# Extra gather moved in among two experts' products, a reordered end of the output stage, and latent products between two condition halves

## The chip, the core and the metric

The kernel runs on one core of one Trainium2 chip. The time is device microseconds (us) of one execution on that core, smaller is better. Before the change the median of three runs is 1278.52 us, from 1276.56 to 1280.14.

## The reference, cut to what matters

Two layers of a transformer-like block work on 256 latent tokens and 256 context tokens of width 1024. In each layer, modulation values come from a condition vector, tokens are normalised and mixed (attention and Fourier branches), and then go through a mixture of experts in which a router picks one of four groups for each token and two of its four experts:

```python
mod = silu_c @ w_ada[l] + b_ada[l]
h_lat = rmsnorm(x_lat, norm1_g[l]) * (1.0 + sc1) + sh1
...
m = g_a * (o_a @ w_br_mla) + g_b * (o_b @ w_br_na) + g_c * (o_c @ w_br_ft)
return m @ w_out
...
x_lat = x_lat + g1 * y_lat
h_lat = rmsnorm(x_lat, norm2_g[l]) * (1.0 + sc2) + sh2
x_lat = x_lat + g2 * grouped_moe(h_lat, router_w, router_bias, w_e_gate[l], w_e_up[l], w_e_down[l])
```

The second layer needs the context only as keys and values, so its output stage and its experts work on the 256 latent tokens alone.

## The kernel before

Everything is float32, and the large products are made of three products of float32r parts: each weight chunk (128 x 2048, 1 MB) is loaded by SyncE into one of five `raw` buffers, ScalarE writes the high part of half a chunk (`half_high`, L557) into one of four `w_hi` buffers, VectorE writes the low part (`half_low`, L937), and TensorE runs `three` (L1574 to L1576) on them. A high part waits until TensorE has used the half four places earlier. There is no scheduler: every engine's order is written out by hand in its own block, and engines wait for each other by semaphores. A result in PSUM lives in one of eight banks; the plan at the top gives each result its bank, and TensorE waits (`claim`) until the bank's last reader has finished.

The change touches three places of this order.

**Opening.** `condition_half` (L1661) makes half of a modulation row from one chunk of `w_ada`. `turn_rows(1)` (L1676) turns the row of the two halves of pair 1 once ScalarE has copied it; VectorE makes the modulation of blocks 2 and 3 from it. `latent(kb)` is the contraction block `kb` of the first input product: 12 products of 512 columns.

**Output stage.** Four passes `j` each make two 128-wide blocks of x. For block `kb`, VectorE adds to x (L1296) and scales a copy `xc` (L1303), ScalarE squares x (L598), and `token_block(kb)` on TensorE adds the router's logits (L1935) and transposes `xc` (L1941) into `tok` banks, for ScalarE to copy. The squares of blocks 0 to 5 are added up in `rinv` by VectorE (L953); those of blocks 6 and 7 stay in `sq`. `sums_of` (L1985) sums `rinv` and both `sq` over the features. `sum_done` is raised by the last logits, and lets ScalarE make the root `rs` (L831), from which VectorE's routing chain starts. `filler` (L2004) are products whose result nobody reads.

**Experts.** Routing puts the tokens into 4 units of 128 slots, one per group, and into extra units for tokens beyond those (3 in the first layer, 1 in the second). `n_it` is the number of experts run: 28, then 20. For expert `i`, `up(i, a)` for `a` = 0 to 3 uses half-chunk `a` (6 products of 512 columns each); then `silu` (ScalarE), `hidden` (VectorE, which scales with the token's gate `gsl`), `turn(i)` (TensorE transposes the hidden values), and `down(i)` (12 products). TensorE issues `up(i, 0)`, `turn(i - 1)`, `up(i, 1..3)`, `down(i - 1)`. The tokens of the first four units are gathered before expert 0, into `h_hi` and `h_lo`. Those of the extra units (`hx_hi`, `hx_lo`) are first read by expert 16. They are gathered in one block between experts 0 and 1:

```python
                for i in range(n_it + 1):
                    if i == 1:
                        b, was = L["row"][0]
                        claim((b, was))
                        pe.wait_ge(diag_done, l + 1)
```

In this block stand the slot numbers (L2154; ScalarE copies them to `sbr`, L894), and for each of the eight blocks `kb` of features the gathering products (L2048, and L2062 in the first layer), with the gates of one unit (L2169) behind the first `n_unit` of them. ScalarE and VectorE make `hx_hi` (L855, L856) and `hx_lo` (L1423, L1424) of each, also all eight in a row; VectorE's `unit_gates` (L1465, L1466) and `hidden(0)` (L1480) stand among them.

## Time and profile before

| | us |
|---|---|
| median of three runs | 1278.52 |
| the profiled execution, its own time | 1281.17 |
| its span, first to last instruction | 1279.5 |
| TensorE busy | 1230.6 (96%) |
| VectorE busy | 858.1 (67%) |
| ScalarE busy | 693.1 (54%) |
| mean granted TensorE clock | 0.983 |

The profiled execution took 1.67 us more than its span. Busy time of TensorE includes products at half the clock. In a timeline row the first number is the start, the second the time to the end of the last instruction, and the brackets hold the idle time of the engine ahead of it with what ended it; consecutive equal instructions are merged ("x4"). A float32 product shows as two instructions, so x8 can stand for four products of the program. PE is TensorE, PEld its weight loads, DVE VectorE, ACT ScalarE.

### The profile page before, as it was taken

The numbers are of one execution on the slowest core, as the hardware profiler recorded it, in microseconds if no ns is written. First come the engines' busy times: TensorE is split into PE (matmuls) and PEld (weight loads), VectorE is DVE, ScalarE is ACT, GpSimd is POOL, SyncE is SP. The second block draws the span as 40 slices with busy tenths as digits, with TensorE's granted clock in tenths as the row PEclk, the third lists the DMA queues.
The fourth block names the chain that finished last, engine by engine and source line by source line (L and its number), as shares of the span: only waits on it lengthen the run. The fifth ranks groups of instructions, "written<-read, shape, count | busy, mean of one in ns | idle before, by whom it ended". The sixth has DMA issues, their size and how long they took to land.

```text
span 1279.5 us, 17771 instructions
## 1 busy us (share of the span) xinstructions
PE 1230.6 (96%) x6762; PEld 978.5 (76%) x6762; DVE 858.1 (67%) x1338; ACT 693.1 (54%) x1043; POOL 15.0 (1%) x28
## 2 busy tenths in 40 slices
PE   6999999999999999999999999999899998999997
PEld 4777555688888886888888887786599986888875
DVE  4653556442444547599998996847665667899986
ACT  4432545533223344488886783536554455788863
POOL 0100000000000000000000000000000000000000
PEclk8999999999999989999999999999999998999998
DMA  9622699422222111399998993321645541899981
GB/s 364 270 88 78 234 390 338 158 99 99 99 99 99 67 66 54 122 373 371 366 364 304 349 365 127 137 99 66 264 140 190 185 145 66 323 369 369 369 305 39
DMA packets 38564, 268.98 MB, mean 210 GB/s; under 512 B 4241, under 2 KB 5393, under 8 KB 6481
## 3 DMA queue, kind: packets, MB, share of 16 engines
q1 hardware_dynamic: 37520, 263.39, 55.8%
q0 software_dynamic: 960, 4.46, 0.9%
q8 instruction: 56, 0.92, 0.3%
q14 instruction: 28, 0.22, 0.1%
HBM read 266.78 MB, written 1.05 MB: 209 GB/s over the span
## 4 chain that ended last, share of the span: by engine, by line
PE 87%; DVE 7%; ACT 2%; issue 1%; DMA 1%; SPq 0%; DVEq 0%; ACTq 0%; PEldq 0%
PE bank L1574 22%; PE bank L1576 22%; PE bank L1575 22%; PE bank L2048 3%; PE bank L1661 3%; PE bank L1841 3%; PE bank L1884 2%; PE bank L1866 2%; DVE lo L937 2%; DMA raw<-weights 1%; PE bank L1935 1%; PE bank L2143 1%; PE bank L2144 1%; PE bank L2113 1%; PE bank L1776 1%
## 5 line engine op out<-in xcount | busy, mean ns | idle before, releaser
L937 DVE TENSOR_TENSOR lo<-raw,w_hi 128x1024 fp32r<-128x1024 f32 x400 | 486.4, 1231 | 211.2 <-ACT w_hi L557 206.8
L557 ACT CAST w_hi<-raw 128x1024 fp32r<-128x1024 f32 x400 | 418.2, 1051 | 264.9 <-PE bank L1576 258.5
L1574 PE MATMUL bank<-h_hi,w_hi 128*128 128x512 f32 (+1 forms) x512 | 177.7, 347 | 4.2 <-DVE h_lo L997 2.1
L1575 PE MATMUL bank<-h_lo,w_hi 128*128 128x512 f32 (+1 forms) x512 | 176.1, 344 | 0.0
L1576 PE MATMUL bank<-h_hi,lo 128*128 128x512 f32 (+1 forms) x512 | 175.8, 343 | 0.0
L1574 PE MATMUL bank<-w_hi,h_hi 128*128 128x512 f32 (+1 forms) x320 | 126.9, 396 | 0.3 <-DVE h_lo L1424 0.2
L1576 PE MATMUL bank<-w_hi,h_lo 128*128 128x512 f32 (+1 forms) x320 | 124.4, 389 | 0.0
L1575 PE MATMUL bank<-lo,h_hi 128*128 128x512 f32 (+1 forms) x320 | 124.3, 389 | 0.0
L1574 PEld LDWEIGHTS bank<-h_hi,w_hi 128*128 128x128 f32 x512 | 97.4, 190 | 21.7 <-issue 5.9
L1576 PEld LDWEIGHTS bank<-h_hi,lo 128*128 128x128 f32 x512 | 97.4, 190 | 11.6
L1575 PEld LDWEIGHTS bank<-h_lo,w_hi 128*128 128x128 f32 x512 | 97.5, 190 | 11.0
L1574 PE MATMUL bank<-w_hi,hdT_hi 128*128 128x512 f32 x192 | 76.0, 396 | 0.0
L1575 PE MATMUL bank<-lo,hdT_hi 128*128 128x512 f32 x192 | 75.9, 395 | 0.0
L1576 PE MATMUL bank<-w_hi,hdT_lo 128*128 128x512 f32 x192 | 75.9, 395 | 0.0
L1574 PEld LDWEIGHTS bank<-w_hi,h_hi 128*128 128x128 f32 x320 | 60.7, 190 | 13.1 <-issue 1.1
L1576 PEld LDWEIGHTS bank<-w_hi,h_lo 128*128 128x128 f32 x320 | 60.6, 189 | 12.5
L1575 PEld LDWEIGHTS bank<-lo,h_hi 128*128 128x128 f32 x320 | 60.6, 190 | 11.6
L1178 DVE TENSOR_REDUCE smx<-bank 128x1 f32<-128x512 f32 (+1 forms) x72 | 42.0, 600 | 26.3 <-PE bank L1841 25.1
L755 ACT ACTIVATE prob<-bank,smx 128x512 f32<-128x512 f32 (+1 forms) x72 | 44.3, 619 | 26.3 <-DVE smx L1178 25.3
L762 ACT COPY probT<-bank 128x512 f32<-128x512 f32 x60 | 32.8, 591 | 39.0 <-PE bank L1866 39.0
L1574 PE MATMUL bank<-w_hi,hx_hi 128*128 128x512 f32 x128 | 51.9, 406 | 0.0
L1661 PE MATMUL bank<-raw,cs 128*32 128x256 f32 x768 | 48.7, 393 | 2.7 <-DMA raw<-weights 2.6
(262 smaller groups left out, 1991.9 us busy)
## 6 DMA issues: line engine op xcount, KB each, us to landing
raw<-weights SPq DMA_DIRECT2D x248, 1024.0 KB, 5.0
x<-tokens SPq DMA_DIRECT2D x4, 512.0 KB, 7.2
nab<-na_bias POOLq DMA_DIRECT2D x2, 1024.0 KB, 8.8
rp<-rope POOLq DMA_DIRECT2D x2, 512.0 KB, 4.3
ft<-dft POOLq DMA_DIRECT2D x2, 512.0 KB, 4.7
out<-x SPq DMA_DIRECT2D x4, 256.0 KB, 2.2
fd<-dft POOLq DMA_DIRECT2D x2, 128.0 KB, 5.5
vec<-vectors SPq DMA_DIRECT2D x1, 176.0 KB, 2.4
```

The lines of the kernel that those rows point to most:

```text
L557: nc.scalar.copy(w_hi[:, g % N_HI, :], raw[:, ring_slot[c], o:o + HALF]).then_inc(hi_done, 1)
L755: nc.scalar.activation(prob[:, i % 2, qb, 0:nk * P], bank[b][:, 0:nk * P], ACT.Exp, bias=smx[:, i % 2, 2 + qb:3 + qb], scale=1.0, accum_ou ...
L762: nc.scalar.copy(probT[:, i % 2, 2 * half:2 * half + 2, :], bank[b][:].rearrange("p (k q) -> p k q", k=2))\
L937: nc.vector.tensor_tensor(lo[:, ring_slot[c], o:o + HALF], raw[:, ring_slot[c], o:o + HALF], w_hi[:, g % N_HI, :].bitcast(F32), ALU.subtra ...
L1178: nc.vector.tensor_reduce(smx[:, i % 2, 2 + qb:3 + qb], bank[b][:, 0:nk * P], AX, ALU.max, negate=True)\
L1574: nc.tensor.matmul(o, l_hi, r_hi, start=start, stop=False)
L1575: nc.tensor.matmul(o, l_hi, r_lo, start=False, stop=False)
L1576: return nc.tensor.matmul(o, l_lo, r_hi, start=False, stop=stop)
L1661: ins = nc.tensor.matmul(o[32 * j:32 * j + 32, :], cs[:, w:w + N_COND], raw[:, ring_slot[p], kb * CW:(kb + 1) * CW], start=(r == 0 and hal ...
L1841: ins = nc.tensor.matmul(bank[b][:, 0:nk * P], q[:, h, t], k[:, h, k0:k0 + nk * P], start=True, stop=True)
L1866: ins = nc.tensor.transpose(bank[b][:, o:o + P], prob[:, i % 2, qb, kb * P:(kb + 1) * P], ident[:])
L2048: ins = nc.tensor.matmul(bank[b][:, 0:c1 - c0], h[:, t, kb * P:(kb + 1) * P], perm[:, t, c0:c1], start=(start and t == 0), stop=last)
```

## The change

1. Opening: `latent(0)` now stands between the two halves of condition pair 1.
2. Output stage: the sum over `rinv` moves ahead, into the last pass, between the first and the second half of its product. At the end of the stage the logits of blocks 6 and 7 and the two remaining sums come first, and the transposes of blocks 6 and 7 last.
3. Experts: the slot numbers and all gates are made during expert 0 (`beside`), and each block of the extra gather stands behind one `up(i, a)` of the experts 1 and 2. ScalarE and VectorE take their parts in the same order. The gates' bank is 5 in place of 3.

The lines of the changed kernel stand 7 to 23 lines further down, so L1935 of before is L1945 there, L1985 is L1966, L2048 is L2071. The diff, cut:

```diff
-            s["gsl"], s["row"] = results(1, [3]), results(1, [6])
+            s["gsl"], s["row"] = results(1, [5]), results(1, [6])
...
+                def extra_high(kb):
+                    b, was = L["gx"][kb]
+                    act.wait_ge(full[b], nth(b, was))
+                    shifted(hx_hi, kb, b, n_ext * P).then_inc(gxhi_done, 1)
...
+                    if i in (1, 2):
+                        extra_high(4 * (i - 1))
...
-                    more(hs[1])
-                    more(hs[2])
+                    for a in (1, 2):
+                        more(hs[a])
+                        if i in (1, 2):
+                            extra_high(4 * (i - 1) + a)
                     silu(i)
+                    if i == 0:
+                        b, was = L["row"][0]
+                        act.wait_ge(full[b], nth(b, was))
+                        nc.scalar.copy(sbr[:, 0:nq], bank[b][:, 0:nq]).then_inc(free[b], 1)
+                    if i in (1, 2):
+                        extra_high(4 * (i - 1) + 3)
                     for g in hs[3:]:
                         more(g)
...
+                def extra_low(kb):
+                    b, was = L["gx"][kb]
+                    dve.wait_ge(gxhi_done, KB * l + kb + 1)
+                    unshifted(hx_lo, hx_hi, kb, b, n_ext * P).then_inc(free[b], 1)
...
-                    if i == 1:
-                        for kb in range(KB):
-                            if kb == n_unit:
-                                unit_gates()
-                                hidden(0)
-                            b, was = L["gx"][kb]
-                            dve.wait_ge(gxhi_done, KB * l + kb + 1)
-                            unshifted(hx_lo, hx_hi, kb, b, n_ext * P).then_inc(free[b], 1)
...
-                    more(hs[1])
-                    more(hs[2])
-                    if i > 0:
-                        hidden(i)
+                    for a in (1, 2):
+                        more(hs[a])
+                        if i in (1, 2):
+                            extra_low(4 * (i - 1) + a)
+                    if i == 0:
+                        unit_gates()
+                    hidden(i)
+                    if i in (1, 2):
+                        extra_low(4 * (i - 1) + 3)
                     for g in hs[3:]:
                         more(g)
...
-                    condition(1)
+                    condition_half(1, 0)
                     latent(0)
+                    condition_half(1, 1)
                     turn_rows(1)
                     latent(1)
...
-                def token_block(kb):
-
-                    b, was = L["tok"][kb]
-                    claim((b, was))
+                def logits(kb):
+
                     if kb == 0:
                         claim((bs, wass))
                     pe.wait_ge(xc_done, KB * l + kb + 1)
...
+                def token_rows(kb):
+
+                    b, was = L["tok"][kb]
+                    claim((b, was))
                     for t in range(nt):
                         ins = nc.tensor.transpose(bank[b][:, t * P:(t + 1) * P], xc[:, kb, t * P:(t + 1) * P], ident[:])
                     ins.then_inc(full[b], 1)
+
+                def token_block(kb):
+
+                    logits(kb)
+                    token_rows(kb)
...
                         if a == 0 and j > 0:
                             token_block(2 * j - 2)
                             token_block(2 * j - 1)
+                            if j == N_OUT - 1:
+                                pe.wait_ge(acc_done, acc_from(2 * l + 2))
+                                sums_of(rinv)
                             if ns == 2 and j >= 2:
                                 shift_rows(j - 2)
                     s += 1
 
-                def sums_of(part):
-                    for t in range(nt):
-                        nc.tensor.matmul(bank[bs][:, t:t + 1], part[:, t * P:(t + 1) * P], ones[:, 0:1], start=False,
-                                         stop=False, skip_group_check=True)
-
                 n = 2 * l + 1
-                pe.wait_ge(acc_done, acc_from(n + 1))
-                sums_of(rinv)
+                logits(KB - 2)
                 pe.wait_ge(nsq_done, KB * n + KB - 1)
                 sums_of(sq[:, 0, :])
-                token_block(KB - 2)
                 pe.wait_ge(nsq_done, KB * n + KB)
                 sums_of(sq[:, 1, :])
-                token_block(KB - 1)
+                logits(KB - 1)
+                token_rows(KB - 2)
+                token_rows(KB - 1)
 
...
-                for i in range(n_it + 1):
-                    if i == 1:
-                        b, was = L["row"][0]
+                def slot_numbers():
+
+                    b, was = L["row"][0]
+                    claim((b, was))
+                    pe.wait_ge(diag_done, l + 1)
+                    for t in range(nt):
+                        ins = nc.tensor.matmul(bank[b][:, t * P:(t + 1) * P], ones[:], diag[:, t, :], start=True, stop=True)
+                    ins.then_inc(full[b], 1)
+
+                def slot_gates(units):
...
-                        claim((bg, wasg))
                         pe.wait_ge(g4_done, l + 1)
                         pe.wait_ge(permx_done, l + 1)
-                        for kb in range(KB):
-                            claim(L["gx"][kb])
-                            gather(L["gx"][kb], htok_hi, kb, 512, n_unit * P, True)
-                            gather(L["gx"][kb], htok_lo, kb, 512, n_unit * P, False)
-                            shifted(L["gx"][kb], kb, 512, n_unit * P)
-                            if kb < n_unit:
-                                for t in range(nt):
-                                    ins = nc.tensor.matmul(bank[bg][:, 8 * kb:8 * kb + 8], perm[:, t, kb * P:(kb + 1) * P],
-                                                           g48[:, t, :], start=(t == 0), stop=(t == nt - 1))
-                            if kb == n_unit - 1:
-                                ins.then_inc(full[bg], 1)
+                    for u_ in units:
+                        for t in range(nt):
+                            ins = nc.tensor.matmul(bank[b][:, 8 * u_:8 * u_ + 8], perm[:, t, u_ * P:(u_ + 1) * P],
+                                                   g48[:, t, :], start=(t == 0), stop=(t == nt - 1))
+                    if units[-1] == n_unit - 1:
+                        ins.then_inc(full[b], 1)
+
+                def gathered_extra(kb):
+
+                    claim(L["gx"][kb])
+                    gather(L["gx"][kb], htok_hi, kb, 512, n_unit * P, True)
+                    gather(L["gx"][kb], htok_lo, kb, 512, n_unit * P, False)
+                    shifted(L["gx"][kb], kb, 512, n_unit * P)
+
+                def beside(i, a):
+
+                    if i == 0 and a == 0 and ns == 2:
+                        slot_rows(1, 512, n_unit * P)
+                    if i == 0 and a == 1:
+                        slot_gates(range(n_unit - 3))
+                    if i == 0 and a == 2:
+                        slot_numbers()
+                        slot_gates(range(n_unit - 3, n_unit))
+                    if i in (1, 2):
+                        gathered_extra(4 * (i - 1) + a)
+
+                for i in range(n_it + 1):
                     for m in back_at(l, i):
                         back(m, range(4), L["back"][m])
                     if i < n_it:
                         up(i, 0)
+                        beside(i, 0)
                     if i > 0:
                         turn(i - 1)
                     if i < n_it:
-                        up(i, 1)
-                        up(i, 2)
-                        up(i, 3)
+                        for a in range(1, 4):
+                            up(i, a)
+                            beside(i, a)
                     if i == n_it:
                         for m in (4, 5):
                             back(m, range(4), L["back"][m])
```

TensorE at the end of the output stage, first layer, before: the last product of the last pass and what follows (`sq` are squares, `xc` the scaled x, `rt` routing values).

```order
L1576 MATMUL bank<-m_hi,lo 128x512
L1985 MATMUL bank<-ones,rinv 128x1 x4
L1985 MATMUL bank<-ones,sq 128x1 x4
L1935 MATMUL bank<-vec,xc 128x16 x4
L1941 MATMUL bank<-ident,xc 128x128 x4
L1985 MATMUL bank<-ones,sq 128x1 x4
L1935 MATMUL bank<-vec,xc 128x16 x4
L1941 MATMUL bank<-ident,xc 128x128 x4
L2004 MATMUL bank<-xc,ident 128x256 x5
L2015 MATMUL bank<-rt,ones 128x20
```

The changed kernel behind the last product of that pass:

```order
L1587 MATMUL bank<-m_hi,lo 128x512
L1945 MATMUL bank<-vec,xc 128x16 x4
L1966 MATMUL bank<-ones,sq 128x1 x8
L1945 MATMUL bank<-vec,xc 128x16 x4
L1956 MATMUL bank<-ident,xc 128x128 x8
L2027 MATMUL bank<-xc,ident 128x256 x5
L2038 MATMUL bank<-rt,ones 128x20
L2040 MATMUL bank<-rt,before 128x16
```

And between the two halves of its product, behind the logits of block 5 (`sh_116` are shift rows):

```order
L1945 MATMUL bank<-vec,xc 128x16 x4
L1956 MATMUL bank<-ident,xc 128x128 x4
L1966 MATMUL bank<-ones,rinv 128x1 x4
L1975 MATMUL bank<-ident,sh_116 4x128 x4
L1585 MATMUL bank<-m_hi,w_hi 128x512
```

One group of sums went ahead of the last half product, and both groups of transposes behind the last logits. TensorE from the last product of expert 0 on, second layer, before (`diag` gives the slot numbers, `g_127` the gates, `htok` the tokens):

```order
L1576 MATMUL bank<-w_hi,h_lo 128x512
L2154 MATMUL bank<-diag,ones 128x128 x2
L2048 MATMUL bank<-perm,htok_hi 128x128 x2
L2048 MATMUL bank<-perm,htok_lo 128x128 x2
L2169 MATMUL bank<-g_127,perm 128x8 x2
L2048 MATMUL bank<-perm,htok_hi 128x128 x2
L2048 MATMUL bank<-perm,htok_lo 128x128 x2
L2169 MATMUL bank<-g_127,perm 128x8 x2
```

The changed kernel, between the third and the fourth half-chunk of expert 0:

```order
L1586 MATMUL bank<-lo,h_hi 128x512
L1587 MATMUL bank<-w_hi,h_lo 128x512
L2177 MATMUL bank<-diag,ones 128x128 x2
L2189 MATMUL bank<-g_127,perm 128x8 x6
L1585 MATMUL bank<-w_hi,h_hi 128x512
```

And in expert 1, from the end of its first half-chunk on (`hid` is the hidden values of expert 0):

```order
L1586 MATMUL bank<-lo,h_hi 128x512
L1587 MATMUL bank<-w_hi,h_lo 128x512
L2071 MATMUL bank<-perm,htok_hi 128x128 x2
L2071 MATMUL bank<-perm,htok_lo 128x128 x2
L2136 MATMUL bank<-ident,hid 128x128 x2
L1585 MATMUL bank<-w_hi,h_hi 128x512
L1586 MATMUL bank<-lo,h_hi 128x512
```

The block is gone: numbers and gates stand within expert 0, and the four narrow products of a gather behind each six wide ones. VectorE at this place, second layer, before:

```order
L1424 SCALAR_TENSOR_TENSOR h_lo<-bank,mod,h_hi 128x512
L937 TENSOR_TENSOR lo<-raw,w_hi 128x1024 x4
L1424 SCALAR_TENSOR_TENSOR hx_lo<-bank,mod,hx_hi 128x128 x5
L1465 COPY gsl<-bank 128x20
L1466 TENSOR_TENSOR gsl<-gsl,bank 128x20
L1480 SCALAR_TENSOR_TENSOR hid<-bank,gsl,s_act 128x256
L1424 SCALAR_TENSOR_TENSOR hx_lo<-bank,mod,hx_hi 128x128 x3
L937 TENSOR_TENSOR lo<-raw,w_hi 128x1024
```

And in the changed kernel:

```order
L1431 SCALAR_TENSOR_TENSOR h_lo<-bank,mod,h_hi 128x512
L944 TENSOR_TENSOR lo<-raw,w_hi 128x1024 x3
L1472 COPY gsl<-bank 128x20
L1473 TENSOR_TENSOR gsl<-gsl,bank 128x20
L1492 SCALAR_TENSOR_TENSOR hid<-bank,gsl,s_act 128x256
L944 TENSOR_TENSOR lo<-raw,w_hi 128x1024 x2
L1499 TENSOR_TENSOR hdT_lo<-bank,hdT_hi 128x256
L1431 SCALAR_TENSOR_TENSOR hx_lo<-bank,mod,hx_hi 128x128
L944 TENSOR_TENSOR lo<-raw,w_hi 128x1024
L1431 SCALAR_TENSOR_TENSOR hx_lo<-bank,mod,hx_hi 128x128
```

The gates and `hid` of expert 0 moved ahead of the fourth of the low parts, and the `hx_lo` went in between later ones.

## Rows read from the trace of the kernel before

**Rows 1.** The page, part 4: the chain that ended last, by engine

```profile
PE 87%; DVE 7%; ACT 2%; issue 1%; DMA 1%; SPq 0%; DVEq 0%; ACTq 0%; PEldq 0%
```

**Rows 2.** Busy times in 50 us of experts: PE, PEld, DVE, ACT, POOL, clock, DMA

```profile
1100.00:1150.00 50.00, 50.00 (x225) 40.59 (x224) 48.24 (x54) 40.91 (x50) 0.00 (x0) 1.00 0.99 368
```

**Rows 3.** Timeline of ScalarE: silu of experts 1 and 2, second layer

```profile
1092.93 0.39 ACT L875 ACTIVATE s_act<-bank 128x256 f32<-128x256 f32 x1 [0.26 <-PE bank L1576]
1101.44 0.39 ACT L875 ACTIVATE s_act<-bank 128x256 f32<-128x256 f32 x1 [0.25 <-PE bank L1576]
```

**Rows 4.** Busy times by microsecond, end of the first layer's output stage

```profile
467.00:468.00 1.00, 1.00 (x11) 1.00 (x10) 1.00 (x2) 0.53 (x1) 0.99 (x1) 0.98 0.67 156
468.00:469.00 1.00, 1.00 (x6) 1.00 (x6) 0.18 (x1) 0.00 (x0) 0.04 (x1) 0.50 0.93 393
...
478.00:479.00 1.00, 1.00 (x7) 0.72 (x6) 0.90 (x5) 1.00 (x2) 0.00 (x0) 0.90 0.00 0
```

**Rows 5.** Timeline at the same place

```profile
465.79 0.95 PE L1985 MATMUL bank<-ones,rinv 128*128 128x1 f32 x8
...
468.79 1.09 PE L1941 MATMUL bank<-ident,xc 128*128 128x128 f32 x4
...
469.68 1.71 PE L1985 MATMUL bank<-ones,sq 128*128 128x1 f32 x8
...
473.15 0.26 ACT L831 ACTIVATE rs<-bank,eps 128x4 f32<-128x4 f32 x1 [5.62 <-PE bank L1935]
```

**Rows 6.** Timeline of the second layer's last pass and its end

```profile
1045.91 0.95 DVE L953 TENSOR_TENSOR rinv<-rinv,sq 128x256 f32<-128x256 f32 x2
...
1049.66 0.50 PE L1985 MATMUL bank<-ones,rinv 128*128 128x1 f32 x4
...
1052.17 0.26 ACT L831 ACTIVATE rs<-bank,eps 128x2 f32<-128x2 f32 x1 [1.37 <-PE bank L1935]
```

**Rows 7.** Timeline of the block between experts 0 and 1, first layer

```profile
508.46 1.06 PE L2154 MATMUL bank<-diag,ones 128*128 128x128 f32 x8
...
510.72 0.94 PE L2048 MATMUL bank<-perm,htok_hi 128*128 128x384 f32 x4 [0.50 <-ACT sbr L894]
...
515.07 0.52 PEld L2169 LDWEIGHTS bank<-g,perm 128*128 128x128 f32 x4 [0.19 <-issue]
...
515.51 0.65 PEld L2048 LDWEIGHTS bank<-perm,htok_hi 128*128 128x128 f32 x4
...
529.51 0.50 PE L1574 MATMUL bank<-w_hi,h_hi 128*128 128x512 f32 x1
```

**Rows 8.** Timeline of the block between experts 0 and 1, second layer

```profile
1073.65 4.62 DVE L937 TENSOR_TENSOR lo<-raw,w_hi 128x1024 fp32r<-128x1024 f32 x4
...
1074.58 0.60 PE L2154 MATMUL bank<-diag,ones 128*128 128x128 f32 x4
...
1076.65 0.41 PE L2048 MATMUL bank<-perm,htok_hi 128*128 128x128 f32 x2 [1.47 <-ACT sbr L894]
...
1077.31 0.42 PE L2048 MATMUL bank<-perm,htok_hi 128*128 128x128 f32 x2
...
1083.07 0.48 DVE L1480 SCALAR_TENSOR_TENSOR hid<-bank,gsl,s_act 128x256 f32<-128x256 f32 x1
...
1084.99 0.73 PE L1574 MATMUL bank<-w_hi,h_hi 128*128 128x512 f32 x1
```

**Rows 9.** Busy times by microsecond, the same block

```profile
1079.00:1080.00 1.00, 1.00 (x7) 1.00 (x6) 0.17 (x1) 0.37 (x1) 0.00 (x0) 0.50 0.00 0
...
1089.00:1090.00 1.00, 1.00 (x6) 0.82 (x5) 0.69 (x1) 0.55 (x2) 0.00 (x0) 0.91 0.00 0
```

**Rows 10.** Opening: timeline of TensorE, and busy times of one microsecond

```profile
23.56 1.93 PE L1661 MATMUL bank<-raw,cs 128*32 128x256 f32 x16 [0.54 <-DMA raw<-weights]
25.42 0.80 PE L1574 MATMUL bank<-h_hi,w_hi 128*128 128x512 f32 x1
...
27.00:28.00 1.00, 1.00 (x5) 0.79 (x4) 0.88 (x1) 0.09 (x1) 0.00 (x0) 0.68 1.06 434
```

27 lines of the change are left out of this document (10 added, 17 removed).

## The prediction

> **What bounds the kernel now.** I read first the chain that ended last: 87% of it is TensorE's own work [rows 1], so only what shortens TensorE's queue, or fills a hole in it, can pay. Then I read the busy times stage by stage. In the experts TensorE is busy for 50 of 50 us at a granted clock of 1.00, with VectorE at 48.2 close behind and the DMA at 368 GB/s [rows 2]; one expert takes 8.51 us from silu to silu [rows 3], and as the first experts after the block keep the same pace as later ones, it is TensorE that sets it. An expert has 36 wide products, so one costs about 0.23 us. What can be gained lies between such stretches, and I read these in the timeline and by single microseconds. The clock is a part of it: at the end of the first layer's output stage it goes from 1.00 to 0.50 (2.4 to 1.2 GHz) at 468.0, behind products with one or 16 columns, and returns at 478.2 [rows 4]; between experts 0 and 1 of the second layer it is 0.50 from 1079 on, behind two waits and narrow gathers, and back at 1089.1, four microseconds into expert 1's wide products [rows 8, 9].
>
> **Opening: 0 us.** Before, the first half of pair 1 left TensorE free at about 23.0, 0.54 us of wait for the second half's chunk ahead of 23.56, and `latent(0)` ran from 25.42 on [rows 10]. Its inputs are ready by 22.4, so it can now start at 22.9, the 1.86 us behind its start that the second half shows. But TensorE is at half clock there until about 27.65 (the row 27 to 28 shows 0.68) [rows 10]: 12 products at about 0.43 us, nearly double their 0.23, make 5.0 us, to 27.9; the second half then takes 0.9 us, to 28.8. `turn_rows(1)` stood behind `latent(0)`, which hid ScalarE's copy of the row (0.6 us and the two signals); now TensorE waits for it, until about 29.5, against 29.3 before. ScalarE's next high part, VectorE's low part and modulation 1 stand in queue behind that copy and come 1.5 us later, which `latent(1)` and condition 2 just cover. If the wide work lifts the clock earlier, up to 1.4 us are won; if a transfer comes late, 0.7 us are lost. I take 0.
>
> **Output stage, first layer: 2.0 us won.** The root waits for TensorE's queue: from the first sum at 465.79 to the root at 473.15 are 7.4 us [rows 5]. A group of four such products takes 0.95 us at full clock and 1.71 at half [rows 5]. Now the `rinv` sums lie ahead of the half product, where their squares have long been added, and delay it by 0.95 us; x, its square and `xc` of block 7 shift with it. Behind the product stand four groups (logits, two sums, logits), 3.8 us at full clock, so the root comes at 465.8 + 0.9 + 3.8 + 0.1 = 470.6, 2.5 us earlier. The transposes (1.09 us for four at half clock [rows 5]) go into the shadow of ScalarE's table load and VectorE's chain, and so do the fillers if they keep up. This holds if the clock is still 1.00 while the groups run: the wide product reaches nearer to them than before, so I expect it to be. If the clock goes as before, the same groups cost about 5.6 us and the gain is 0.9; and the narrow groups in the middle of the last pass (logits, transposes, shift rows), to which the sums add 0.95 us without a wide product, may take the clock from the wide products behind them; I price that by what the half clock costs expert 1 now, 1.8 us (below). Between 0.7 and 2.6, I take 2.0, nearer the upper.
>
> **Output stage, second layer: 0.6 us lost.** Here the clock stays, and the sums filled the time in which x and its square of block 7 were made: TensorE's `rinv` sums take 0.50 us at 1049.66, just behind the product [rows 6]. Moved ahead they are on the path. They wait too: VectorE ends the adding of square 5 at 1046.86 [rows 6], and TensorE is there at 1046.7, so about 0.2 us of wait, and the half product with all behind it is 0.7 us later. The transposes taken out give back 0.1 to 0.2, as the last sum must wait for the square. The root that came at 1052.17 [rows 6] comes at about 1052.7. Bounds: 0 and 0.8 lost.
>
> **Experts, first layer: 0 us.** The block lasts from 508.46 to 529.51, 21.05 us [rows 7], all of it TensorE busy but a 0.50 us wait for the copy of `sbr` [rows 7]. One gather costs 1.97 us (513.10 to 515.07, from the page of weight loads) and the gates of one unit 0.44 (515.07 to 515.51) [rows 7]. The work is the same afterwards: 8 x 1.97 for gathers, 7 x 0.44 for gates, 2.0 for numbers and rows make 20.8. The wait goes, and sixteen changes between narrow and wide products come; a change costs between nothing and 0.1 us (the first wide product behind the block takes 0.50 [rows 7]). ScalarE and VectorE have room: a gather adds 0.56 us to VectorE and 2 to TensorE. From 1.1 lost to 0.7 won; I take 0.
>
> **Experts, second layer: 6.6 us won.** From the end of expert 0 (1074.58) to the first product of expert 1 (1084.99) pass 10.4 us [rows 8]. A gather of four products with the gates takes 0.66 us while the clock is 1.00 (1076.65 to 1077.31) [rows 8], without gates 0.45 to 0.5. The rest are the 1.47 us wait for `sbr` [rows 8], waits for the first `hx_lo`, for VectorE first makes four low parts (4.62 us [rows 8]), and half clock from 1078.9. Afterwards: numbers and gates in expert 0, 0.6 + 5 x 0.22 = 1.7 us, of which about 0.4 falls into holes where TensorE waited for `h_lo`: 1.3. Eight gathers at 0.5: 4.0. `turn(0)` needs `hid` of expert 0, which VectorE makes behind three low parts (1073.65 + 3.5), the gates (0.4) and itself (0.48 [rows 8]): 1078.1, against 1077.9 when TensorE gets there; 0.3 of wait. So 10.4 - 5.6 = 4.8. And expert 1 no longer begins at half clock: of the 4.1 us up to 1089.1 [rows 9], half less what its narrow turn takes, 1.8. The sum is 6.6. If the clock falls here all the same, the gain is at most 4.8; if gathers cost 0.44 and no wait is left, 7.6.
>
> The TensorE page of the Trainium skill (TensorE: Matmul & The Clock Gate, "A second HAM failure mode: psum-queue depth-cycling") says that going through PSUM banks in turn leaves short idle times between groups, and the clock then goes back and forth. That speaks against this change, which puts one more bank into the turn. The rows say otherwise so far: the experts already go through six banks at 1.00 for 50 us. The same page's advice ("Avoid throughput drops mid-kernel", under "Why this matters for your kernels") names gaps without products as what to avoid; by it the narrow products alone would cost no clock, but at 468 it fell with TensorE busy for 1.00 of each microsecond [rows 4], so the measurement decides. By that advice the 1.8 us would come only from the waits that go.
>
> **Sum.** 0 + 2.0 - 0.6 + 0 + 6.6 = 8.0 us. Against the profiled execution's 1281.17 that gives 1273.2; that execution lies 2.65 above the median of the runs, so for the median I forecast 1278.52 - 8.0 = 1270.5.
>
> **The rivals.**
> - The clock is taken in a new place, once or twice: in the wide products of the last pass (from about 461), at the first gathers, or in expert 1, each at the 1.8 us that it costs expert 1. For it: all work after the opening shifts by some microseconds, and narrow groups stand closer in the pass. Then 8.0 less 1.8 to 3.6: 1272.3 to 1274.1.
> - VectorE becomes the bound in experts 1 and 2 of the second layer. It is at 48.2 of 50 [rows 2] and gets 0.35 us per gather; before, it made four low parts ahead while TensorE gathered. Against it: TensorE's stretch per half-chunk grows by 0.5, more than VectorE's. If TensorE waited 0.5 us in each of the eight gaps and had to wait for `hid` longer, 5 us of the 6.6 would go: about 1275.5.
> - Slower: bank cycling, or wide and narrow products in turn, holds the clock at 0.50 through experts 1 and 2. In the first layer these last 33 us now and in the second 21; their 144 wide products would cost 0.2 us more each, 29 us: about 1299. It decides from 16 us at half clock on, where the gain is used up. Against it stand the turns and bank changes of every expert at 1.00.
> - The moves hide nothing new: interleaved gathers at 0.66 to 1 us each and a wait at every change. Then the gain is below 1 us, about 1278.
> - More than forecast: the opening wins its 1.4 and the first layer its 2.6, and the second layer its 7.6: 1267 to 1268.5.
>
> **How the numbers follow.** Forecast (1268.7 to 1272) 0.58; clock taken elsewhere 0.20; VectorE 0.09; slower 0.04; nothing 0.04; more 0.05. The limits of 0.3% are 3.8 us, about what a measurement tells here: faster than 1274.7 are the forecast, the clock case, the last one and a part of VectorE's, 0.85; within 0.3%, 0.10; slower 0.05. The range from 1266.5 to 1275.0 takes in the bounds of all terms and the clock case; the runs of before alone spread by 3.6 us.
>
> **What would show it.** In the profile of the changed kernel the root at the end of the first layer's output stage should stand 3.9 us behind the wide products, not 7.4, with the granted clock still 1.00; in the second layer 2.35, not 2.5. From the last product of expert 0 to silu 2 of the second layer, 26.9 us before [rows 3, 8], should be about 19, with no microsecond of half clock. Wrong it would be by half clock within experts 1 and 2, by a wait of over 1 us ahead of `turn(0)`, or by waits for low parts between the gathers.

## The result: 4.7 us less in the first comparison, 7.2 in the second

Forecast were 1270.5 us. In the first comparison the changed kernel took 1274.05 us (median of five runs, 1272.38 to 1274.30) against 1278.79 for the kernel before (median of five, 1276.56 to 1281.06): a ratio of 0.9963, 95% interval 0.9948 to 0.9979, or 4.7 us. Run once more with the first experiments it took 1271.62 against 1278.85, ratio 0.9942 (0.9922 to 0.9962), 7.2 us. By means the two comparisons give 5.2 and 7.3 us, about 6.3 where 8.0 were forecast. The experiments below were run in three sets, each with its own runs of the kernel before, 64 together, whose means lie between 1277.7 and 1279.4; so a kernel is compared only with those beside it. The ratios are estimated from all runs of a comparison and can differ from the quotient of its two medians by up to 0.0014.

The two profiled executions are 8.8 us apart, 1281.17 and 1272.38. That is no contradiction: the first lies above all five runs of its kernel in that comparison and the second is the shortest of its own. The mean granted clock (the share of full speed that TensorE was given) moves with the time. It is 0.984 over the 64 runs before, 0.988 over those of the changed kernel, and among the 64 a straight line through time and clock falls by 0.8 us for each 0.001. Four thousandths is about what the change itself takes away: 10.2 us at half clock between experts 0 and 1 of the second layer (below) are 0.0040 of the mean over 1279 us. By that line a rise of 0.0043 goes with 3.5 us.

**The profile after.** The chain of waits is TensorE's as before, 88% against 87% [rows 1]:

```profile
PE 88%; DVE 7%; ACT 2%; issue 1%; DMA 1%; DVEq 0%; SPq 0%; ACTq 0%; PEldq 0%
```

End of the first layer's output stage, timeline (answers to [rows 5]):

```profile
467.50 0.39 PE L1587 MATMUL bank<-m_hi,lo 128*128 128x512 f32 x1
...
467.73 0.96 PE L1945 MATMUL bank<-vec,xc 128*128 128x16 f32 x8
...
468.54 2.03 PE L1966 MATMUL bank<-ones,sq 128*128 128x1 f32 x16
...
470.43 1.04 PE L1945 MATMUL bank<-vec,xc 128*128 128x16 f32 x8
...
471.32 1.07 PE L1956 MATMUL bank<-ident,xc 128*128 128x128 f32 x8
...
471.51 0.26 ACT L831 ACTIVATE rs<-bank,eps 128x4 f32<-128x4 f32 x1 [2.05 <-PE bank L1945]
```

and the busy times of the same microseconds (answer to [rows 4], the clock is the third number from the right):

```profile
468.00:469.00 1.00, 1.00 (x12) 1.00 (x11) 0.96 (x3) 0.17 (x1) 0.05 (x1) 1.00 0.36 66
471.00:472.00 1.00, 1.00 (x11) 1.00 (x11) 0.18 (x1) 0.47 (x2) 0.00 (x0) 1.00 0.89 377
```

From the first narrow product behind the wide ones at 467.73 to the root are 3.8 us, where they were 7.4 (0.8 us of this are the `rinv` sums, which now stand ahead of the half product); the transposes stand behind the last logits and the clock is at 1.00. In the second layer (answers to [rows 6]) the same distance is 2.3 us, 1048.16 to 1050.45 (2.5 before):

```profile
1048.04 0.28 PE L1587 MATMUL bank<-m_hi,lo 128*128 128x256 f32 x1
1048.16 0.51 PE L1945 MATMUL bank<-vec,xc 128*128 128x16 f32 x4
1048.52 0.58 PE L1966 MATMUL bank<-ones,sq 128*128 128x1 f32 x4
1049.34 0.61 PE L1966 MATMUL bank<-ones,sq 128*128 128x1 f32 x4 [0.24 <-ACT sq L598]
...
1050.45 0.26 ACT L831 ACTIVATE rs<-bank,eps 128x2 f32<-128x2 f32 x1 [1.16 <-PE bank L1945]
```

Experts 0 to 3 of the second layer, timeline (answers to [rows 8] and [rows 3]; the last two rows are silu 2 and silu 3):

```profile
1075.03 0.33 PE L2071 MATMUL bank<-perm,htok_hi 128*128 128x128 f32 x2
...
1075.76 0.48 DVE L1492 SCALAR_TENSOR_TENSOR hid<-bank,gsl,s_act 128x256 f32<-128x256 f32 x1
...
1076.39 0.41 PE L2136 MATMUL bank<-ident,hid 128*128 128x128 f32 x2 [0.81 <-DVE hid L1492]
...
1092.22 0.39 ACT L880 ACTIVATE s_act<-bank 128x256 f32<-128x256 f32 x1 [0.46 <-PE bank L1587]
1101.19 0.39 ACT L880 ACTIVATE s_act<-bank 128x256 f32<-128x256 f32 x1 [0.25 <-PE bank L1587]
```

and busy times (answer to [rows 9]):

```profile
1079.00:1080.00 1.00, 1.00 (x7) 0.83 (x6) 0.75 (x2) 0.59 (x2) 0.00 (x0) 1.00 0.98 147
1089.00:1090.00 1.00, 1.00 (x6) 0.79 (x5) 0.79 (x3) 0.93 (x2) 0.00 (x0) 1.00 1.00 221
```

No block is left; the one wait of TensorE is 0.81 us ahead of the turn, and the clock is 1.00 all through. Expert 0's products end at about 1073.7, so the silu of expert 2 at 1092.22 comes 18.5 us later (26.9 before, about 19 forecast). The opening (answers to [rows 10], timeline of TensorE):

```profile
24.38 0.50 PE L1585 MATMUL bank<-h_hi,w_hi 128*128 128x512 f32 x1 [2.35 <-DVE h_lo L1004]
...
28.68 1.28 PE L1672 MATMUL bank<-raw,cs 128*32 128x256 f32 x16
30.67 1.05 PE L1687 MATMUL bank<-pick,rows 128*128 128x2 f32 x8 [0.72 <-ACT rows L613]
```

The latent products do stand ahead of the second half now, where they waited 2.35 us for VectorE's `h_lo`, and the turn of the rows waits 0.72 us for the copy.

### The profile page after: what moved, and what is told of

The parts are those of the page before. It is cut to its first block, busy times and chain, and to the rows that moved or that the text cites. A ratio compares the mean times of both kernels' runs of the same rounds, so it can differ in the third digit from the quotient of the medians.

```text
span 1270.7 us, 17757 instructions
## 1 busy us (share of the span) xinstructions
PE 1223.3 (96%) x6762; PEld 973.0 (77%) x6762; DVE 857.5 (67%) x1338; ACT 692.2 (54%) x1043; POOL 14.9 (1%) x28
## 4 chain that ended last, share of the span: by engine, by line
PE 88%; DVE 7%; ACT 2%; issue 1%; DMA 1%; DVEq 0%; SPq 0%; ACTq 0%; PEldq 0%
PE bank L1585 22%; PE bank L1587 22%; PE bank L1586 22%; PE bank L1672 3%; PE bank L2071 3%; PE bank L1853 3%; PE bank L1878 2%; PE bank L1896 2%; DVE lo L944 2%; PE bank L2166 1%; PE bank L2136 1%; PE bank L2167 1%; PE bank L1945 1%; PE bank L1788 1%; PE bank L1687 1%
## 5 line engine op out<-in xcount | busy, mean ns | idle before, releaser
L1586 PEld LDWEIGHTS bank<-lo,h_hi 128*128 128x128 f32 x320 | 60.3, 188 | 11.1
L1587 PE MATMUL bank<-w_hi,hx_lo 128*128 128x512 f32 x128 | 50.6, 395 | 0.0
```

Of the source, the lines that this page charges most:

```text
L1586: nc.tensor.matmul(o, l_hi, r_lo, start=False, stop=False)
L1587: return nc.tensor.matmul(o, l_lo, r_hi, start=False, stop=stop)
```

## The experiments

**A measure for all of them.** One profile can't be compared with another as a whole, since the clock falls at other places each time, so I cut each into stages at instructions that every kernel has (starts in the timeline): opening, up to the end of the first latent products; "out", from an output stage's first product to its root; "experts", from the first product of expert 0 to silu 3. "Rest" is the span without these five. Microseconds; e1 to e12 are the experiments below, in which "spread" means the change's gathers:

```
kernel                      opening  out 1  experts 1  out 2  experts 2   rest     span
before                        56.6   61.6     49.8     31.4     41.7    1038.4   1279.5
changed                       57.7   58.8     49.0     31.7     34.6    1038.9   1270.7
e1  experts only              56.4   59.2     49.0     31.6     34.6    1042.4   1273.2
e2  output only               56.1   58.8     49.7     31.9     41.6    1040.4   1278.6
e3  opening only              57.1   61.2     49.8     31.6     41.7    1036.2   1277.5
e4  changed again             57.5   58.8     49.0     33.5     34.6    1036.0   1269.4
e5  block, early numbers      57.8   58.8     50.4     31.7     41.9    1039.8   1280.5
e6  opening as before         54.6   58.8     49.0     33.4     34.6    1040.8   1271.2
e7  sums ahead in layer 1     56.3   58.8     49.0     31.3     34.6    1038.8   1268.8
e8  sums behind in both       57.8   60.6     49.0     31.3     34.6    1035.2   1268.5
e9  two blocks                56.9   58.8     50.3     33.5     42.1    1037.7   1279.3
e10 spread, late numbers      55.2   58.8     48.9     33.2     35.8    1040.8   1272.6
e11 e7 with opening before    54.1   58.8     49.0     31.3     34.6    1038.8   1266.6
e12 e7 again                  53.4   58.8     49.0     31.1     34.6    1037.4   1264.3
```

Where an edit is the same, the four inner stages are the same to 0.3 us unless the clock falls in them; the opening is not (see e6 and e11). "Rest" holds no edit and still goes from 1035.2 to 1042.4. It is 355.0 to 359.7 us between the opening and the first output stage, 464.9 to 470.1 between silu 3 of the first layer and the second output stage (with 0 us at half clock in e8 and 13.7 in e2 and e5), and three stretches that stay: 29.7 from the first root to expert 0, 16.1 to 16.2 from the second, and 169.4 to 169.5 behind silu 3 (168.5 in e12). So nearly all of the noise of "rest" sits in two stretches, and goes with the falls of the clock there.

**e1 to e3: one part of the change each, and e4: the changed kernel again.** They are the hunks of the diff applied alone. e1:

```diff
+                    if i in (1, 2):
+                        gathered_extra(4 * (i - 1) + a)
```

> Before with only the experts' part of the change (the extra gather spread over experts 1 and 2, its bank, the copies on ScalarE and VectorE with it). Theory: the gain sits here, in the second layer's block between experts 0 and 1. It keeps its 6.6 us or nearly (the two profiles show about 7), so that this kernel comes 4 to 7 us under before, median about 1273, and from the last product of expert 0 to silu 2 of the second layer about 19 us. Rival (the experts' part gives less over several executions, since the half clock that the block had is taken elsewhere): 3 us or less, about 1276, with a stretch at 0.50 inside an expert or in the block in the profile.

1273.07 against 1278.85, 5.8 us; the ratio is 0.9944 (0.9922 to 0.9966), or 7.2. The theory holds: experts 2 of the table falls from 41.7 to 34.6 and experts 1 from 49.8 to 49.0. Its mean of 1273.0 lies 0.9 over that of e4, the changed kernel beside it.

e2:

```diff
+                logits(KB - 2)
...
+                logits(KB - 1)
+                token_rows(KB - 2)
+                token_rows(KB - 1)
```

> Before with only the new order at the end of the output stage. Theory: 2.0 won in the first layer less 0.6 in the second, so 1.4 us under before, about 1277.4. Rival (the sums ahead of the half product and the narrow groups cost more than the order behind it gives, and the gap of 3.3 us to the forecast is lost here): 0 to 2 us over before, about 1279 to 1281, with half clock inside the last pass of an output stage or the root of the second layer more than 1 us late.

1279.11 over twelve runs, ratio 0.9999 (0.9983 to 1.0015): nothing, between the two cases. The first layer's stage is 2.8 us shorter than before's and yet the runs don't show it. e1 tells part of why. It has the old order at this place, and its clock stayed until the root (it fell 0.2 us behind it, at 475.4):

```profile
471.00:472.00 1.00, 1.00 (x12) 1.00 (x11) 0.96 (x3) 0.60 (x1) 0.49 (x1) 1.00 0.68 115
474.00:475.00 1.00, 1.00 (x11) 1.00 (x11) 0.00 (x0) 0.00 (x0) 0.00 (x0) 1.00 0.49 205
```

```profile
470.29 0.94 PE L1996 MATMUL bank<-ones,rinv 128*128 128x1 f32 x8
...
472.89 0.63 PE L1952 MATMUL bank<-ident,xc 128*128 128x128 f32 x4
...
473.36 0.95 PE L1996 MATMUL bank<-ones,sq 128*128 128x1 f32 x8
...
475.25 0.26 ACT L831 ACTIVATE rs<-bank,eps 128x4 f32<-128x4 f32 x1 [3.22 <-PE bank L1946]
```

The stage then took 59.2, against 58.8 with the new order: all that leaves the way to the root is one group of transposes, 472.89 to 473.36. So at full clock the order is worth 0.4 us, and the other 2.4 are a fall of the clock that the execution in [rows 4] had and e1 had not. Of the four profiles with the `rinv` sums behind the product, three have it (below).

e3:

```diff
-                    condition(1)
+                    condition_half(1, 0)
                     latent(0)
+                    condition_half(1, 1)
```

> Before with only the opening's order (the latent products of unit 0 between the two halves of condition pair 1). Theory: 0, between 0.7 lost and 1.4 won, about 1278.8. Rival (the opening loses, since the turn of the rows now waits for ScalarE's copy, 0.72 us in the changed kernel's profile, and modulation 1 comes later): 1 to 2 us over before, about 1280, with latent(1) starting over 1 us later than before's, measured from the end of the first turn of rows.

1278.40 over twelve runs, ratio 0.9986 (0.9973 to 0.9998), so 0.3 to 3.5 us faster, while its profile has the opening no shorter (57.1). The wait of 0.7 us ahead of the second turn is there, as in all nine profiles with the new opening, and `latent(1)` starts 11.8 us behind the end of the first turn of rows, against 11.1 before. Runs and profile point in different directions; see e6 and e11.

By means e1, e2 and e3 are 6.4, 0.0 and 1.4 us under the kernel before, together 7.7; the whole change beside them (e4) is 7.3 under.

> The changed kernel once more, nothing edited, for its spread and for a second profiled execution. Theory: the parts cost what the first profile shows, and only the clock's falls differ from execution to execution; the median comes within 1 us of 1274.05, and a profile that lies above 1273.5 has more half clock than the first (whose granted clock was 0.991), at other places, and nothing else that is longer. Rival: a wait or a transfer differs between executions; then the longer one shows a stage that is over 1 us longer at the same clock.

1271.62, outside the 1 us that I had allowed, so five or six runs fix a median less well than I thought. Its profile lies below 1273.5, so it can't test the second half as that was put; but the one edited stage that is over 0.2 us longer than in the first profile is longer by its clock. It is the second layer's output stage, 33.5 against 31.7. Busy times, and the timeline of TensorE there:

```profile
1042.00:1043.00 1.00, 1.00 (x8) 0.98 (x8) 0.00 (x0) 0.65 (x3) 0.00 (x0) 0.90 0.00 0
1043.00:1044.00 1.00, 1.00 (x7) 1.00 (x6) 0.00 (x0) 0.00 (x0) 0.00 (x0) 0.50 0.00 0
```

```profile
1041.16 0.62 PE L1945 MATMUL bank<-vec,xc 128*128 128x16 f32 x4
1041.63 0.41 PE L1956 MATMUL bank<-ident,xc 128*128 128x128 f32 x2
1042.03 0.61 PE L1966 MATMUL bank<-ones,rinv 128*128 128x1 f32 x4
1042.49 0.36 PE L1585 MATMUL bank<-m_hi,w_hi 128*128 128x256 f32 x1
...
1043.44 0.41 PE L1587 MATMUL bank<-m_hi,lo 128*128 128x256 f32 x1
```

Behind the rinv sums, now in the middle of the last pass, the half product's steps cost about 0.21 us each instead of 0.12, for 3.4 us.

**e5: numbers and gates early, the eight gathers in one block.**

```diff
                 for i in range(n_it + 1):
+                    if i == 1:
+                        for kb in range(KB):
+                            gathered_extra(kb)
...
-                    if i in (1, 2):
-                        gathered_extra(4 * (i - 1) + a)
```

> The changed kernel with its eight extra gathers put back in one block ahead of expert 1 (high and low parts with them); slot numbers, gates, the copies and the hidden rows of expert 0 stay early, in expert 0. In the second layer before takes 41.7 us from the first product of expert 0 to silu 3, the changed kernel 34.6. Theory (waits behind a queue and the half clock that follows them make the 7.1): the 1.47 us wait for the copy and the wait behind four low parts are gone and eight gathers at 0.5 to 0.66 stand in a row; if the clock stays at 1.00 the stretch takes 35 to 36.5 us and the gathers' spreading is worth only 1 to 2 us; median within 2 us of the changed kernel, 1272.8. Rival (a block of narrow products takes the clock by itself): 0.50 again near 1080, the stretch takes 38 us or more, median 3 us or more over the changed kernel.

1279.40 against 1277.18, ratio 1.0006 (0.9994 to 1.0019): all of the gain is gone. The numbers are those of the rival, but my theory fell in its first half already: the waits did not go, so this run does not show that a block of narrow products takes the clock by itself. The block (timelines of TensorE and VectorE):

```profile
1077.06 0.44 PE L2065 MATMUL bank<-perm,htok_hi 128*128 128x128 f32 x2 [0.74 <-ACT sbr L919]
...
1080.21 0.55 PE L2065 MATMUL bank<-perm,htok_hi 128*128 128x128 f32 x2 [2.04 <-DVE hx_lo L1428]
```

```profile
1074.46 3.48 DVE L941 TENSOR_TENSOR lo<-raw,w_hi 128x1024 fp32r<-128x1024 f32 x3
...
1078.28 0.48 DVE L1489 SCALAR_TENSOR_TENSOR hid<-bank,gsl,s_act 128x256 f32<-128x256 f32 x1
1078.68 1.21 DVE L941 TENSOR_TENSOR lo<-raw,w_hi 128x1024 fp32r<-128x1024 f32 x1
1079.81 0.60 DVE L1428 SCALAR_TENSOR_TENSOR hx_lo<-bank,mod,hx_hi 128x128 fp32r<-128x128 f32 x2
```

TensorE comes to its third gather, whose bank is free only when `hx_lo` has been made, and VectorE is still at the weights' low parts and the hidden rows in its queue. Before, the 1.47 us wait for the copy [rows 8] had covered that, and 0.46 us of it was left. With the copy earlier it is 2.04 (and 0.74 of wait for the copy is left, as ScalarE makes it behind silu 0). The 0.50 stands again from 1080.4 to 1090.6:

```profile
1081.00:1082.00 1.00, 1.00 (x5) 0.84 (x4) 0.35 (x1) 0.37 (x1) 0.00 (x0) 0.50 0.00 0
```

**e9: two blocks of four gathers.**

```diff
                 for i in range(n_it + 1):
+                    if i in (1, 2):
+                        for kb in range(4 * (i - 1), 4 * i):
+                            gathered_extra(kb)
```

> The changed kernel with the extra gathers in two blocks: four right ahead of expert 1's up products, four ahead of expert 2's, instead of one behind each quarter. The one block of eight (e5) took 41.9 us from the first product of expert 0 to silu 3 of the second layer, with 2.04 us of wait for the second bank's low part, 0.74 for the first, and 0.50 from 1080 on; the changed kernel takes 34.6. Theory (a block waits because VectorE still has weights' low parts in its queue, and the wait with narrow work behind it takes the clock): the first block waits as long as before, and the stretch takes 38 to 40 us. Rival (the length of the narrow stretch takes the clock, and four gathers are short enough): 0.91 to 1.00 all through and 35 to 37 us.

1280.96 against 1279.00, ratio 1.0009 (0.9999 to 1.0019), the stretch 42.1: worse than either case. TensorE waits 0.74 and 2.02 us in the first block and 1.87 in the second:

```profile
1078.81 0.44 PE L2065 MATMUL bank<-perm,htok_hi 128*128 128x128 f32 x2 [2.02 <-DVE hx_lo L1428]
...
1092.76 0.44 PE L2065 MATMUL bank<-perm,htok_hi 128*128 128x128 f32 x2 [1.87 <-DVE hx_lo L1428]
```

```profile
1080.00:1081.00 1.00, 1.00 (x3) 0.81 (x4) 0.61 (x2) 0.37 (x1) 0.00 (x0) 0.50 0.08 16
...
1094.00:1095.00 1.00, 1.00 (x5) 0.81 (x5) 0.56 (x2) 0.37 (x1) 0.00 (x0) 0.50 0.26 107
```

The clock is at 0.50 for 6.8 us here and 10.2 in e5 and before, and the stretch is no shorter. A sum fits: idle time of TensorE plus half of the half-clock time is 2.2 + 5.1 = 7.3 before, 2.8 + 5.1 = 7.9 in e5, 4.6 + 3.4 = 8.0 in e9, and 0.8 in the changed kernel. The differences from the changed kernel, 6.5, 7.1 and 7.2, stand against measured 7.1, 7.3 and 7.5. Whether a block without any wait would keep the clock, no run shows.

**e10: gathers spread, numbers and gates late.**

```diff
                 for i in range(n_it + 1):
+                    if i == 1:
+                        slot_numbers()
+                        if ns == 2:
+                            slot_rows(1, 512, n_unit * P)
+                        slot_gates(range(n_unit))
```

> The changed kernel with its gathers spread as it has them, but slot numbers, slot rows and gates in one piece at the start of expert 1, with ScalarE's copy, the gates and the hidden rows of expert 0 behind them, as before had them. Theory (the gathers' spreading is what pays, since e5 with early numbers and a block gained nothing): the second layer's stretch from the first product of expert 0 to silu 3 takes 34.6 to 36 us, the median within 1.5 us of the changed kernel. Rival (both are needed, as the turn of expert 0 now waits for gates and hidden rows behind VectorE's low parts, and narrow products stand in a row): a wait of 1 us or more ahead of the turn, half clock in it, and 37 us or more.

1271.03 against 1279.00, ratio 0.9931 (0.9917 to 0.9944); the stretch takes 35.8, 1.2 more than in the changed kernel. The wait ahead of the turn is there and takes no clock with it:

```profile
1078.35 0.41 PE L2138 MATMUL bank<-ident,hid 128*128 128x128 f32 x2 [1.15 <-DVE hid L1492]
```

With e5 this settles what each part of the experts' change is worth. Early numbers alone bring nothing, spread gathers alone 5.9 of the 7.1 us, and early numbers the last 1.2 once the gathers are spread. (The waits explain 0.5 of these: 1.15 and 0.2 us here, 0.81 in the changed kernel.)

**e7, e8, e12: where the rinv sums stand.** e7 keeps them ahead of the half product in the first layer alone; e8 has them behind it in both:

```diff
-                            if j == N_OUT - 1:
+                            if j == N_OUT - 1 and l == 0:
```

> The changed kernel, but in the second layer the rinv sums stand behind the half product again, where they filled a wait; the logits and transposes keep the new order. From the first product of the output stage to its root the second layer takes 31.4 to 31.6 us with the old order and 31.7 to 31.9 with the new. Theory (moving them there costs 0.2 to 0.3): the stretch falls back to 31.4 to 31.6 and the median is 0 to 0.5 us under the changed kernel, which the runs will hardly tell. Rival (the narrow groups in the middle of the last pass take the clock there, as in one profile of the changed kernel, 1.7 us): no half clock in this stretch and 0.5 to 1.5 us under the changed kernel.

> The changed kernel with the rinv sums behind the half product in both layers; logits first and transposes last stay. Theory (only the transposes out of the way and a clock that holds make the first layer's gain): first layer from the first product of the output stage to its root 58.8 to 59.2 us at full clock, as the sums cost their 0.95 at either place; the half clock may come back at about 468, then 61 us. Rival (the sums' place is what pays): 59.5 us or more at full clock, and the median 0.7 us or more over the changed kernel.

> The kernel of e7 once more, for its spread beside the three others. Theory: ratio to before within 0.0015 of 0.9931, the second layer's output stage 31.4 to 31.6 us where the clock stays. Rival (e7 was a lucky set, its falls of the clock few): ratio 0.995 or more, as the changed kernel has it.

e7: 1270.11 against 1277.18, ratio 0.9931 (0.991 to 0.9953). e12, the same kernel beside other ones: 1270.72 against 1279.00, 0.9929 (0.9916 to 0.9942). e8: 1270.23, 0.9943 (0.9924 to 0.9962). The profiles say more than these intervals, which overlap with each other and with e4's. With the sums in the middle of the second layer's last pass (changed, e2, e4, e5, e6, e9, e10) the clock fell there in four of seven, and the stage takes 31.7 to 31.9, or 33.2 to 33.5 with the fall. With the sums behind the product (before, e1, e3, e7, e8, e11, e12) it fell in none of seven: 31.4 to 31.6 with the old order, 31.1 to 31.3 with logits first and transposes last. In the first layer the sums' place does matter the other way: ahead of the product the stage took 58.8 in all ten profiles, behind it 59.2 once and 60.6 to 61.6 three times, each of these with 0.50 from between 468.0 and 469.5 on. e8's 60.6 is the second case of its theory. e7's ratio lies 0.0011 under that of e4, 1.4 us, which is the case of its rival (the narrow groups take the clock), and the count of four in seven against none in seven says the same; e12 confirms its ratio, and its stage of 31.1 is a little better than foretold. A fall of the clock behind the root costs nothing here: in e7, e10 and e12 it came 0.6 to 1.1 us behind it, and from the root to expert 0 pass 29.7 us in all fourteen profiles.

**e6 and e11: the opening as before.**

```diff
-                    condition_half(1, 0)
+                    condition(1)
                     latent(0)
-                    condition_half(1, 1)
```

> The changed kernel with the opening of before. Six profiles give from the first root to the end of latent products 41.1 to 42.1 us with either opening. Theory (the opening is worth 0): within 0.7 us of the changed kernel, 1272.1 to 1273.5. Rival (it pays by itself, as the opening alone came out 1 us under before on the mean of twelve runs): 1 to 1.5 us over the changed kernel, about 1274.

> The kernel of e7 (changed kernel, rinv sums ahead of the half product in the first layer alone) with the opening of before. Theory (at equal half clock the new opening is 0.4 to 0.9 us later at the second turn of rows: 10.7 to 10.9 us from the first against 10.2 to 10.8, and 9.6 against 8.8): 0.3 to 1 us under e7 run beside it. Rival (the new opening gains over many runs, as alone it came out 1 us under before): 0.5 to 1.5 us over e7.

e6 came to 1271.59, ratio 0.9949 (0.9925 to 0.9973), between the changed kernel's two, as the theory of no effect has it. One of e11's six runs lasted 2419.56 us and is in no ratio; why is not known. The median of the other five is 1269.41, ratio 0.9928 (0.9904 to 0.9951), beside 1270.72 and 0.9929 for e12; their means are 1269.95 and 1269.62: neither of the two cases, rather no difference. The opening's stage is 53.4 to 57.8 long in nine profiles with the new order, mean 56.6, and 54.1 to 56.6 in five with the old, mean 55.6; within an order it moves by up to 4.4 us. Half of the 1.1 us between the means stands ahead of the first edited line (the first turn of rows starts at 18.8 on average with the new order, at 18.3 with the old). From that turn to the end of the latent products, profiles with the same 6.8 us at half clock take 38.7 to 38.9 us with the new order (e3, e7, e9) and 38.2 to 38.7 with the old (before, e1, e2). So the stages have it 0 to 0.7 us slower and e3's runs have it faster: what the new opening is worth I can't tell from zero.

## Where the forecast was right and where it was off

- **Experts, second layer (6.6 forecast).** Right, and a little too small: 7.1 in each of eight profiles with the change's gathers and numbers. Numbers and gates cost 0.8 us (expert 0's products take 7.1 us, 6.3 before) and not 1.3, and TensorE came to the turn that much sooner. But the working had the wrong share for the 1.47 us wait: e5 shows that when it goes, VectorE's queue puts 2.04 us in its place, and only the wide products between gathers cover that queue. The wait ahead of the turn was 0.8, not 0.3 (its own terms give 1078.0 against 1077.9, so 0.1).
- **The half clock there.** Right: none in experts 1 and 2, in any of nine profiles with spread gathers, and 0.50 in all five without. The Trainium skill (TensorE: Matmul & The Clock Gate, "A second HAM failure mode: psum-queue depth-cycling") tells of another kernel in which cycling through PSUM banks made the clock go back and forth. In the experts of this one no such thing shows.
- **Experts, first layer (0).** Low: 0.8 won in all nine profiles with spread gathers, the upper bound of 0.7 and a little over. The sixteen changes between narrow and wide products cost nothing that shows.
- **Output stage, first layer (2.0).** Near, against the profile it was made from (2.8), and unsure as a term for the median. The weak step is that I took the half clock of [rows 4] as a part of every execution. At full clock the order is worth 0.4 (e1); three profiles with the order of before (two with the fall, one without) average 60.7, so about 1.9, but on three profiles that rests. e2's twelve runs show nothing of it; with the loss in the second layer they should show 0.8, and their interval, 2.2 us faster to 1.9 slower, can't tell that from zero.
- **Output stage, second layer (0.6 lost).** Mis-sized the other way. The order costs 0.2 us at full clock and about 1.8 with the fall that came with it in four of seven profiles, so 1.1 on average. I had named this rival, narrow groups in the last pass that take the clock at 1.8 us, but for the first layer's pass. It came in the second.
- **Opening (0).** Latent products did move ahead, in the profile not to 22.9 but to 24.38: the first turn of rows came at 20.1 in place of 18.1, behind products that took nearly twice their time (below), and with it `h_lo`, for which TensorE waited. In the five profiles with the new order and no such start they begin at 21.7 to 22.6. The turn's wait for the copy came as forecast. What the opening is worth stays open.
- **The sum.** By stage means the change is 1.9 - 1.1 + 0.8 + 7.1 = 8.7 us without the opening. The runs show 4.7 (2.7 to 6.6 by the ratio's interval) and 7.2 (4.9 to 10.0), so the second comparison allows 8.7 and the first does not. That 8.7 lies so near the 8.0 is in part luck: the first layer's experts and the second layer's output stage were missed by 0.8 and 0.5 in opposite directions. What keeps the runs below it is not settled. If most executions of the kernel before keep their clock in the first output stage, as e1 did, the sum is 7.2; no run shows how often they do. "Rest" does not take it: its mean is 1038.8 in the nine profiles with spread gathers and 1038.5 in the five others.
- **The rivals.** "The clock is taken in a new place" (1272.3 to 1274.1) came in four of seven profiles, with the place off by a layer, and takes 1.6 us where it comes; I gave it 0.20 and should have put its mean into the sum. The first median, 1274.05, lies in its range and the second, 1271.62, in that of the forecast (1268.7 to 1272), but the first comparison's own profile has no fall there, so the range alone shows nothing. VectorE as the bound did not come (one wait of 0.81 us), nor did the slower case.

A better version follows: the changed kernel with the rinv sums ahead of the half product in the first layer only (e7 and e12, ratios 0.9931 and 0.9929). None of the four profiles with the sums behind the product and the new order (e7, e8, e11, e12) has the second layer's fall. The intervals don't separate it from the changed kernel's 0.9942; what speaks for it is the stage, 31.1 to 31.3 us against 32.7 on average.

## What to carry to other kernels

When the consumers of narrow products share a queue with other work, try these products between wide ones: here a block made TensorE wait for that queue even with its inputs earlier, and taking one wait away only uncovered the next. Work that fills a wait is free where it stands; moved into a stretch of wide products it cost its time here, and in four of seven profiles the clock of what follows. Before a half-clock stretch is booked as a gain, look whether several executions have it at that place: book it at its frequency.

## What the runs showed of the hardware

- The clock fell in unedited code too. In the first layer's attention the stage from the latent products to the output stage takes 354.9 to 355.0 us in ten profiles, 356.6 in three with a fall near 205, and 359.7 in e1 with two:

```profile
206.00:207.00 1.00, 0.49 (x4) 0.36 (x6) 0.96 (x3) 0.59 (x2) 0.00 (x0) 0.50 0.96 393
237.00:238.00 1.00, 0.94 (x6) 0.65 (x8) 0.06 (x1) 0.91 (x1) 0.00 (x0) 0.50 1.01 426
```

- The granted clock in the rows can't be trusted in the first microseconds. The first clock record of the changed kernel's trace stands at 18.9 us, and a row ahead of it reads 1.00. Here is that of 16 to 17 us; yet the 32 products around it take 3.49 us, against 1.93 for 32 of the same shape at 34.5:

```profile
16.00:17.00 1.00, 1.00 (x16) 0.42 (x12) 0.86 (x2) 0.07 (x1) 0.00 (x0) 1.00 1.05 442
```

```profile
15.70 3.49 PE L1672 MATMUL bank<-raw,cs 128*32 128x256 f32 x32
...
34.51 1.93 PE L1672 MATMUL bank<-raw,cs 128*32 128x256 f32 x32
```

Five of fourteen profiles have their first record at 18.7 to 19.0 us and take 3.3 to 3.6 us for these products; in the other nine it stands at 11.2 to 15.0 and they take 1.9 to 2.6. The first turn of rows behind them starts at 19.9 to 20.2 us in the five and at 17.4 to 18.3 in the nine.
- A wait of 1.15 us behind one gather, with wide products around (e10), took no clock. One of 2 us in a block of gathers (e5, e9) was followed by 0.50 within a microsecond. Waits are not needed for it: at 468 of the kernel before, behind products of one and 16 columns, TensorE had been busy for 1.00 of each microsecond from 461 on, and in e4 the last wait, 0.41 us, had ended 2.4 us before the clock fell. The order of e4 kept its clock at this place in three of seven profiles.
